# A two-layer transformer forward pass: small stages of layer two moved beside another product, bias rows written once, and fences parted

## The reference, cut to what matters

```python
h = rms_norm_2(x, ln1_w)
proj = h @ w_in                      # q 1024, six k/v of 256, gates 24, qkv 3072, z 1024, a 8, b 8, merge 4096
# compressed attention branch: 32 tokens flattened (+ position), two small matrices
blocks = blocks + pe
flat = blocks...reshape(b, n_cmp, g, CMP_BLOCK * dh)     # 15 blocks, 2 groups, 32*128 long
kc = jax.nn.gelu(flat_k @ w1_k) @ w2_k                   # hidden 256
vc = jax.nn.gelu(flat_v @ w1_v) @ w2_v
```

## Time and profile before

| | |
|---|---|
| Median of three executions | 3448.09 us |
| The profiled execution | 3446.6 us |
| Its span | 3444.8 us |
| TensorE busy | 3072.5 us, 89% of the span |
| VectorE, ScalarE busy | 1596.7 us, 1312.6 us |
| Mean granted TensorE clock | 0.926 of full |
| DMA moved | 519.30 MB, mean 151 GB/s |

### The profile page before, as it was taken

One profiled execution on the slowest core, in us unless ns is written; L12 is line 12 of the kernel. 1 busy time (PEld: TensorE's weight loads), 2 busy tenths in 40 slices (PEclk: granted clock), 3 DMA queues, 4 the chain that ended last, 5 costly groups with the idle time before them and its releaser, 6 DMA issues.

```text
span 3444.8 us, 36204 instructions
## 1 busy us (share of the span) xinstructions
PE 3072.5 (89%) x14022; PEld 2525.0 (73%) x14022; DVE 1596.7 (46%) x1648; ACT 1312.6 (38%) x1404; POOL 48.0 (1%) x89
## 2 busy tenths in 40 slices
PE   6798874998999999998997888799889999999997
PEld 5686554876887778776885676688768887888785
DVE  3332335455554445544424556444455544444443
ACT  3333231354443334434333334422233444334432
POOL 0001000000000000000001000000000000000000
PEclk9897775999999999999988999898999999999998
DMA  7643120543554455445525333222345555555553
GB/s 180 193 171 101 49 82 11 195 159 111 184 186 151 175 194 184 151 171 189 197 90 189 121 110 123 109 94 85 149 158 183 183 186 180 188 188 185 178 188 110
DMA packets 78180, 519.30 MB, mean 151 GB/s; under 512 B 10048, under 2 KB 10260, under 8 KB 24544
## 3 DMA queue, kind: packets, MB, share of 16 engines
q1 hardware_dynamic: 71280, 485.64, 39.2%
q0 software_dynamic: 6800, 32.28, 3.7%
HBM read 505.56 MB, written 12.32 MB: 150 GB/s over the span
## 4 chain that ended last, share of the span: by engine, by line
PE 82%; DVE 6%; ACT 4%; DMA 3%; issue 2%; DVEq 1%; ACTq 0%; another core or an unknown queue 0%; SPq 0%; POOL 0%; POOLq 0%; PEldq 0%
PE acc L282 24%; PE acc L284 23%; PE acc L283 23%; DMA w_raw<-in_w_win 2%; DVE w_lo L194 2%; PE wk L618 1%; ACT w_hi L189 1%; PE wk L649 1%; PE wk L1222 1%; PE wk L1128 1%; PE wk L1800 1%; PE wk L632 1%; ACT h_hi L441 1%; PE wk L1798 1%; PE wk L621 1%
## 5 line engine op out<-in xcount | busy, mean ns | idle before, releaser
L194 DVE TENSOR_TENSOR w_lo<-w_raw,w_hi 128x2048 fp32r<-128x2048 f32 (+2 forms) x492 | 1061.1, 2157 | 1257.9 <-ACT w_hi L189 1257.7
L189 ACT ACTIVATE w_hi<-w_raw 128x2048 fp32r<-128x2048 f32 (+2 forms) x492 | 889.2, 1808 | 1220.3 <-PE acc L284 1136.6
L282 PE MATMUL acc<-w_hi,h_hi 128*128 128x512 f32 x2656 | 1071.4, 403 | 102.1 <-DVE w_lo L194 45.7
L283 PE MATMUL acc<-w_lo,h_hi 128*128 128x512 f32 x2656 | 1055.1, 397 | 0.0
L284 PE MATMUL acc<-w_hi,h_lo 128*128 128x512 f32 x2656 | 1053.6, 397 | 0.0
L282 PEld LDWEIGHTS acc<-w_hi,h_hi 128*128 128x128 f32 x2656 | 515.1, 194 | 226.6 <-issue 64.2
L284 PEld LDWEIGHTS acc<-w_hi,h_lo 128*128 128x128 f32 x2656 | 513.9, 193 | 110.0
L283 PEld LDWEIGHTS acc<-w_lo,h_hi 128*128 128x128 f32 x2656 | 515.1, 194 | 104.0
L282 PE MATMUL acc<-w_hi,f_hi 128*128 128x512 f32 x856 | 341.5, 399 | 14.9 <-DVE x L330 7.0
L284 PE MATMUL acc<-w_hi,f_lo 128*128 128x512 f32 x856 | 339.6, 397 | 0.0
L283 PE MATMUL acc<-w_lo,f_hi 128*128 128x512 f32 x856 | 337.3, 394 | 0.0
(11 more groups left out here) (359 smaller groups left out, 2169.6 us busy)
## 6 DMA issues: line engine op xcount, KB each, us to landing
w_raw<-in_w_up_a SPq DMA_DIRECT2D x76, 1024.0 KB, 4.8
w_raw<-in_w_up_b SPq DMA_DIRECT2D x72, 1024.0 KB, 4.8
w_raw<-in_w_win SPq DMA_DIRECT2D x52, 1024.0 KB, 4.8
w_raw<-in_w_merge SPq DMA_DIRECT2D x32, 1024.0 KB, 4.8
w_raw<-in_w_down_a SPq DMA_DIRECT2D x32, 1024.0 KB, 4.8
w_raw<-in_w_down_b SPq DMA_DIRECT2D x32, 1024.0 KB, 4.8
w_raw<-in_w_win2g SPq DMA_DIRECT2D x24, 1024.0 KB, 4.8
w_raw<-in_w_down_a SPq DMA_DIRECT2D x24, 768.0 KB, 4.2
```

The source lines that it names most:

```text
L189: act_.activation(w_hi[:, s % SPL, 0:k], w_raw[:, s % RAW, 0:k], ACT.Copy).then_inc(hi_ready, 1)
L194: dve_.tensor_tensor(w_lo[:, s % SPL, 0:k], w_raw[:, s % RAW, 0:k], w_hi[:, s % SPL, 0:k].bitcast(F32), ALU.subtract).then_inc(lo_ready, 1)
L282: pe_.matmul(o, xh, wh, start=kt == 0, stop=False)
L283: pe_.matmul(o, xh, wl, start=False, stop=False)
```

## The change

It does these things:
- `win2` has the compression columns first (chunk 0), then q (chunks 1 and 2), then the other k (chunk 3) and v (chunk 4).
- `win2` is a Together with `small2`, the turning in three stages, and `flat` in two parts; the items after which the 9 parts stand are given by hand. `cmp_k`, `cmp_v` follow, in 4 items of the full 1 MB each. `z` comes behind them, beside `compress` in 3 parts.
- A fence is parted, in every Together: the signal is given when the last part of a small stage is done, the wait stands ahead of the first part of the next.
- A bias row is stored once in HBM, and a second DMA, HBM to HBM, makes the 128 copies, with 128 as its outer dimension and all heads in one row; the loads of `tri` and `cmask` stand between them.

```diff
-P2_Q, P2_KC, P2_VC, P2_KS, P2_KW, P2_VS, P2_VW = 0, 1024, 1280, 1536, 1792, 2048, 2304
+P2_KC, P2_VC, P2_Q, P2_KS, P2_KW, P2_VS, P2_VW = 0, 256, 512, 1536, 1792, 2048, 2304
...
-        ("win2", 5, four, CH), ("cmp_k", 1, split_counts(32, 8), CHID), ("cmp_v", 1, split_counts(32, 8), CHID),
-        ("win2g", 6, four, CH), ("z", 2, four, CH),
+        ("win2", 5, four, CH), ("cmp_k", 1, [8] * 4, CHID), ("cmp_v", 1, [8] * 4, CHID),
+        ("z", 2, four, CH), ("win2g", 6, four, CH),
...
-        toe1 = nc.dram_tensor("toe1_scratch", (A_H, P, TOE), F32, kind="Internal").ap()
-        toe2 = nc.dram_tensor("toe2_scratch", (N_H, P, TOE), F32, kind="Internal").ap()
+        row1 = nc.dram_tensor("toe1_rows", (A_H, TOE), F32, kind="Internal").ap()
+        row2 = nc.dram_tensor("toe2_rows", (N_H, TOE), F32, kind="Internal").ap()
+        toe1 = nc.dram_tensor("toe1_scratch", (P, A_H * TOE), F32, kind="Internal").ap()
+        toe2 = nc.dram_tensor("toe2_scratch", (P, N_H * TOE), F32, kind="Internal").ap()
...
+                self.slots = slots or [-(-(p + 1) * Q // self.parts) - 1 for p in range(self.parts)]
...
             def pieces(self, k, e):
                 for i, w in enumerate(self.work):
-                    yield from w.walk(k, e)
-
-                    e.drain().then_inc(fenced[k], 1)
                     for other in fenced:
-                        if other != k:
-                            e.wait_ge(fenced[other], self.base + i + 1)
+                        if i and other != k:
+                            e.wait_ge(fenced[other], self.base + i)
+                    parts = w.walk(k, e)
+                    for p in range(w.parts):
+                        next(parts)
+                        if p == w.parts - 1:
+                            for _ in parts:
+                                pass
+                            e.drain().then_inc(fenced[k], 1)
+                        yield
...
-                        g.pe_item(e, n, j, False)
+                        g.pe_item(e, n, j, n == 0)
...
-                        make(ahead[q + 1][0], e, ahead[q + 1][1], ahead[q + 1][2])
-                    while done < (q + 1) * self.parts // Q:
+                        if q or not g.norm:
+                            make(ahead[q + 1][0], e, ahead[q + 1][1], ahead[q + 1][2])
+                        if q == 1 and g.norm and k == "act":
+                            g.norm.root(e, 1)
+                        if q == 1 and g.norm and k == "dve":
+                            g.norm.inverse(e, 1).then_inc(scaled, 1)
+                    while done < self.parts and self.slots[done] <= q:
...
-            for table, row, heads in ((toe1, tsum[0], A_H), (toe2, tsum[1], N_H)):
-                e.dma_start(table, row.unsqueeze(1).to_broadcast([heads, P, TOE])).then_inc(toe_dma, 16)
-            e.wait_ge(toe_dma, 32)
+            for rows, row in ((row1, tsum[0]), (row2, tsum[1])):
+                e.dma_start(rows, row).then_inc(toe_rows, 16)
             load(e, "tri", tri[:], t_in["tri"])
             load(e, "cmask", cmask[:], t_in["cmask"])
+            e.wait_ge(toe_rows, 32)
+            for table, rows, heads in ((toe1, row1, A_H), (toe2, row2, N_H)):
+                every = bass.AP(tensor=rows.tensor, offset=0, ap=[[0, P], [1, heads * TOE]])
+                e.dma_start(table, every).then_inc(toe_dma, 16)
+            e.wait_ge(toe_dma, 32)
...
-                    src = bass.AP(tensor=table.tensor, offset=h * P * TOE + off, ap=[[TOE - 1, P], [1, w]])
+                    src = bass.AP(tensor=table.tensor, offset=h * TOE + off, ap=[[heads * TOE - 1, P], [1, w]])
...
-        stages.append(Gemm("win2", lhs, 0, *rows_to(p2, norm=ln1.norm)))
-        stages[-1].follows(ln1)
-        stages.append(spilled)
+        win2 = Gemm("win2", lhs, 0, *rows_to(p2, norm=ln1.norm))
+        win2.follows(ln1)
...
+        def turn2(name, chunk, first, tiles):
+            ...
+            def pe_after(e):
+                for t in range(TT):
+                    e.wait_ge(evac[t], win2.c + chunk + 1)
+                yield from pe(e)
...
-        stages.append(Together("small2+z", [Gemm("z", lhs, 0, *rows_to(z_rows, norm=ln1.norm))], [
-            small2, turn2, Steps("flat", None, flat_act, flat_dve)]))
+        stages.append(Together("win2+small2", [win2], [
+            small2, turn2("turn_kv_c", 0, P2_KC, range(8, 12)), Steps("flat", None, flat_act, flat_dve, 2),
+            turn2("turn_q", 2, P2_Q, range(0, 8)), turn2("turn_k", 3, P2_KS, range(12, 16))],
+            [4, 5, 6, 8, 9, 10, 13, 14, 17]))
+        stages.append(spilled)
...
-        stages.append(Steps("compress", cmp_pe, cmp_act, None))
+        stages.append(Together("z+compress", [Gemm("z", lhs, 0, *rows_to(z_rows, norm=ln1.norm))],
+                               [Steps("compress", cmp_pe, cmp_act, None, 3)], [0, 2, 4]))
```

More of the change, by code:

```diff
@@ L363, in build, with __init__ @@
         class Together:
-            def __init__(self, name, gemms, work, lead=0):
+            def __init__(self, name, gemms, work, slots=None):
                 self.name, self.gemms, self.work = name, gemms, work
@@ L370, in __init__ @@
                 self.parts = sum(w.parts for w in work)
-                self.lead = lead
+                Q = sum(g.n * g.ipc for g in gemms)
+                self.slots = slots or [-(-(p + 1) * Q // self.parts) - 1 for p in range(self.parts)]
+                assert len(self.slots) == self.parts and self.slots == sorted(self.slots)
                 self.base = fences[0]
@@ L389, in run @@
                 make = Gemm.make_hi if k == "act" else Gemm.make_lo
-                work, done, Q = self.pieces(k, e), 0, len(items)
+                work, done = self.pieces(k, e), 0
                 for q, (g, n, j) in enumerate(items):
                     if k == "pe":
-                        g.pe_item(e, n, j, False)
+                        g.pe_item(e, n, j, n == 0)
                     else:
@@ L1481, in build @@
         small2 = Steps("small2", small2_pe, small2_act, small2_dve, 3)
-        turn2 = Steps("turn2", *to_tiles([
-            ((lambda t, i=i: p2[:, t, i * P:(i + 1) * P]), tt2[:, i, :]) for i in range(16)]))
+        def turn2(name, chunk, first, tiles):
+            pe, act, dve, parts = to_tiles([
+                ((lambda t, c=first + i * P: p2[:, t, c:c + P]), tt2[:, tile, :]) for i, tile in enumerate(tiles)])
+            def pe_after(e):
+                for t in range(TT):
+                    e.wait_ge(evac[t], win2.c + chunk + 1)
+                yield from pe(e)
+            return Steps(name, pe_after if parts > 1 else lambda e: list(pe_after(e)), act if parts > 1 else lambda e: list(act(e)), dve, parts)
         after_turn2 = len(stages) + 1
@@ L1512, in flat_dve @@
                 if k:
+                    yield
+                if k:
                     e.wait_ge(f_hi_s, 2 * k)
@@ L1532, in flat_act @@
                 act_.activation(flat_hi[:, k * FW:(k + 1) * FW], lp2[:, 0:FW], ACT.Copy).then_inc(f_hi_s, 1)
+                if not k:
+                    yield
             act_.activation(flat_hi[:, 2 * FW:2048], lp2[:, 1100:1100 + 2048 - 2 * FW], ACT.Copy)
+            yield
         z_rows = x[:, :, 0:1024]
-        stages.append(Together("small2+z", [Gemm("z", lhs, 0, *rows_to(z_rows, norm=ln1.norm))], [
-            small2, turn2, Steps("flat", None, flat_act, flat_dve)]))
+        stages.append(Together("win2+small2", [win2], [
[3 more added lines that the diff above has]
+        stages.append(spilled)
         class Compress(Gemm):
@@ L2184, in layout @@
     mg = o[12]
-    weights("win2", cols(w, [(q, 1024), (kc, 256), (vc, 256), (ks, 256), (kw, 256), (vs, 256), (vw, 256)]))
+    weights("win2", cols(w, [(kc, 256), (vc, 256), (q, 1024), (ks, 256), (kw, 256), (vs, 256), (vw, 256)]))
     weights("win2g", cols(w, [(qkv, 3072)]))
```

3 lines of the change are left out of this document (2 added, 1 removed).

## The result

The changed kernel takes **3386.24 us** in the median of four executions (3382.98 to 3391.24); the kernel before, beside it on the same chip, 3447.24 us (3444.63 to 3448.18). The ratio is 0.9826, with a 95% interval from 0.9808 to 0.9843: 61 us less. The prediction was 3393 us, in a range of 3380 to 3414. The profiled execution took 3388.2 us with a span of 3386.3, which is 58.4 us less than the profiled execution before. Where they differ by a few microseconds, the traces of the other runs tell what comes back each time and what doesn't; experiment 7 has a second one of the changed kernel.

A forecast was written before the change was run, and what follows sets the result against it. TensorE, busy nine tenths of most slices, was taken as the bound, so only its waits or low clock could give time back. 3446.6 - 33 - 19 - 3 = 3391.6, with the median 1.5 us higher: 3393 us, range 3380 to 3414.

The forecast's parts named there:

- Bias rows: In `win`: 34.2 us lost while the bias rows were stored, less 1 us of stall, a gain of 33 us.
- rival 1: In `win`: the HBM to HBM copy still starves it, gain 12 instead of 33, 3414 us; chance 0.13.
- rival 3: In `win`: a copy from one row is served from one place in memory and runs longer, 3467 us; chance 0.03.
- The other sum of the prediction: Bias copy in `win`: 16 engines at an unchanged rate each, a copy of 53 us and a gain of 9.
- Layer two: From `win2` to `win2g`: moved small stages and full compression items gain 19 us, from 7 to 25.
- item 8: In `win2`: ScalarE does the last part of `small2` before rounding this item, a new wait losing 1.4 us.
- `flat`: Two parts behind items 9 and 10 of `win2`: waits of 2.6 and 2.1 us, net gain 5.4 us.
- clock: In `win2`: lower clock behind the three new waits, between nothing and 3 x 1.8 us, taken as 2.0 lost.
- compression products and `compress`: `cmp_k`, `cmp_v` in full items, 7.5 us a pair, gain 8.6 us; `compress` beside `z`, gain 2.9 us.
- sign of error: In the profile of layer two: `win2` longer than 157 us would show the forecast wrong.
- second price for the three waits: In `win2`: by the skill's clock rule each wait costs, 5.4 us instead of 2.0, and the sum is 3396.
- The fences elsewhere: Parted fences in `gdn+merge` (2.3 us there) and all other Togethers: 3 us together, bounds 0 and 8.

The follow-up runs named there:

- experiment 7: Changed kernel with `flat` in three parts instead of two: 3380.71 us; repeated on one chip 3380.03 us, beside the unedited changed kernel at 3385.25 us.
- experiment 4: Kernel before, bias rows stored once in HBM and copied from there in the old layout's 1.5 KB pieces, 128 outermost: 3413.43 us.
- experiment 5: Kernel before, bias rows stored once in HBM and copied from there in 1.5 KB pieces, the heads outermost: 3410.75 us.
- experiment 1: Kernel before with only the bias rows' part of the change: 3409.15 us, ratio 0.9894.
- experiment 3: Changed kernel with the old fences, signal and wait together ahead of the next small stage: 3389.94 us, ratio 0.9843.
- experiment 2: Kernel before with only the parted fences: 3436.10 us over ten executions, ratio 0.9972.

## Why the prediction was right, step by step

**Bias rows, 33 us predicted.** 34.5 in the trace, 37 by themselves in the runs. The sum said 1 us of stall, and there is none. The reason that I gave, long pieces and repeated reads of one row that aren't slow, needs mending. Pieces of 1.5 KB are as good when they come from HBM (experiments 4 and 5). I had weighed shape and traffic, and the source decided. So the size came out by a comparison with copies of another kind, and that is partly luck. Rivals 1 and 3 both priced the traffic at the HBM; it costs nothing here. The other sum of the prediction, 9 us of gain by the rule of the Trainium skill on the number of engines (DMA: Bandwidth & Descriptors, Why a DMA increments its semaphore by 16 and not by 1) and an unchanged rate of an engine, is far off, because the packets themselves became 3.7 times faster in experiment 5. (By the first store's rate, 2304 KB over 12 engines in 41.2 us, that sum gives 51.5 us for the copy and not 53, and rival 1's 54% is 0.56 in the row of `win2`; neither changes the argument.)

**Layer two, 19 us predicted, 17.1 in the trace.** By its terms:

| | predicted | trace |
|---|---|---|
| `win2`, `z` and `flat` (waits in `z` 5.3, item 8 -1.4, `flat` 5.4, clock -2.0) | 7.3 | 207.7 - 158.0 - 43.5 = 6.2 |
| compression products and `compress` (8.6 and 2.9) | 11.5 | 45.8 - 31.4 - 3.4 = 11.0 |

43.5 are `z`'s eight items and 3.4 the rest of its window. Item 8 waited 1.38 us against 1.4, item 11 2.85 against 2.6. Item 12 waited 0.35 and not 2.1, because item 11 ran slower: its 7.2 us at the lower clock gave VectorE 1.8 us more. In the second trace, at full clock, it waited 1.79. Wait and clock were not independent, as my sum had them: 2.85 + 0.35 + 1.8 = 5.0 us in one trace and 2.84 + 1.79 = 4.6 in the other stand against 2.6 + 2.1 and a part of 2.0. Experiment 7 takes 4.6 of them away in either pair and so shows what they were worth.

A pair of items in `cmp` took 7.49 us, from the second wait to the third here, where 7.5 were predicted:

```profile
1745.63 0.38 PE L284 MATMUL acc<-w_hi,oa_hi 128*128 128x256 f32 x1 [1.44 <-DVE w_lo L196]
1753.12 0.39 PE L284 MATMUL acc<-w_hi,oa_hi 128*128 128x256 f32 x1 [1.45 <-DVE w_lo L196]
```

That is the filling and the pair as foretold; both products took 31.4 us, just above the 31 that I had named.

What my sum had wrong is the length of the small product. I carried it over from one execution: with the 8-column matmuls 29.0 us to the next item, and 7.1 for that item. In the changed trace they took 31.0 and 8.2, which is why `win2` took 158.0 us, above the 157 that I had named as a sign of error; by the terms of my sum it was to take 155.3. The move is not the cause. In four other traces of the old place they took 31.4 to 32.3 us to the next item, in seven others of the new place 29.8 to 30.3. The 29.0 were the shortest of all thirteen. In the second trace of the changed kernel `win2` took 157.2. `z` with `compress` took 47.1 us in both, 1.5 less than the 48.6 of my sum, which hides a part of it. From the first matmul of `win2` to that of `win2g` were 253.3 us before, 256.5 to 257.3 in the three runs with only the bias rows changed, and 236.3 and 235.6 in the two traces of the changed kernel. So layer two's gain is 17 to 22 us by the pair of traces that one takes, and 19.2 by the medians of experiments 1 and 3.

**Rule and rows on the clock.** The prediction's second price for the three waits, 5.4 us, was my reading of the Trainium skill (TensorE: Matmul & The Clock Gate, Part 1: The HAM clock gate), which says that the throttled clock is the default and activity releases it; that each short wait pays, it doesn't say. It came out too high. Behind the wait of 1.38 us the clock is 1.00, and six waits of 0.6 to 1.5 us in `cmp` leave it at 1.00. Behind the wait of 2.85 us stands a low stretch, and behind the same wait of 2.84 us in the second trace none. That the clock falls where TensorE stands for long agrees with the old `flat` and `compress`, at 0.68 and 0.70; what a short wait costs can't be told from its length here.

**The fences elsewhere, 3 us.** From attention's end on the trace gives 1.2 us, but in that part 5.3 us are chance: the stretch from attention's end into `gdn+merge`, with the same code and the same waits of TensorE, took 121.9 us here, at a clock of 0.89, and 116.5 in the second trace of the changed kernel, at 0.95. Behind it the rows are steady (the two last lines of the table): together 404.0 to 404.5 us in the five traces with old fences, 401.2 to 401.6 in seven of the eight with the new ones and 403.1 in the eighth. Between the five and the seven that is 2.4 to 3.3 us, so the 3 us were right. What fell is the expectation of experiment 2, 3 to 5 us for the fences alone: it counted the next item's remainder made ahead of a drain, and left out what an earlier start of `flat` and Gelu, and a clock that stays up in `z`, bring where they stand in the open.

**What the sum lacked.** The start of `win2g`, 2 us. The pair of traces has 5.3 us between `win2g`'s first items and the end of attention: 194.5 us before and 189.2 now. Windows of `win2g`'s start and of the rest, before, then after:

```profile
1871.50:1884.00 12.50, 12.50 (x47) 10.13 (x48) 3.33 (x6) 5.69 (x7) 1.06 (x2) 0.81 0.29 100
1884.00:2066.00 182.00, 159.46 (x744) 129.62 (x743) 95.96 (x215) 70.80 (x145) 0.00 (x0) 0.92 0.32 116
```

```profile
1819.30:1830.00 10.70, 10.55 (x48) 8.81 (x49) 3.59 (x7) 5.70 (x7) 1.06 (x2) 1.00 0.55 202
1830.00:2008.50 178.50, 155.98 (x742) 127.14 (x741) 95.72 (x215) 70.76 (x145) 0.00 (x0) 0.94 0.33 118
```

1.8 us come from `win2g`'s start: in the old order it stood behind `compress` in the open and began at the lower clock. The other 3.5 go with a clock of 0.94 for 0.92 at equal work. Which of the two comes back shows in the lengths of the same stretches, from a start of `w_lo` to another, in us (the times are those of the kernel before):

| | before | experiments 1, 4, 5 | 2, fences alone | changed | changed, second trace | 3, old fences |
|---|---|---|---|---|---|---|
| layer two, 1596 to 1874 | 277.9 | 281.8, 282.4, 280.8 | 275.0 | 261.4 | 258.8 | 260.2 |
| `win2g`'s start, to 1884 | 9.9 | 10.2, 9.9, 9.1 | 9.9 | 7.8 | 7.9 | 8.0 |
| attention, to 2066 | 182.7 | 179.8, 182.7, 179.4 | 180.0 | 179.5 | 182.1 | 180.7 |
| start of `gdn+merge`, to 2187 | 120.9 | 120.8, 120.9, 119.1 | 119.5 | 121.9 | 116.5 | 116.4 |
| `gdn+merge`, to 2393 | 205.5 | 205.4, 205.5, 204.5 | 201.6 | 201.7 | 202.0 | 205.5 |
| its end and what follows, to 2591 | 198.6 | 198.6, 198.5, 200.0 | 199.6 | 199.9 | 199.4 | 198.9 |

The start of `win2g` is shorter in every trace of the new order. Attention is not: it takes 179.4 to 182.7 us in the old order and 179.0 to 185.3 in all eight traces of the new one. Its 3.5 us are chance of these two executions.

## What to carry to other kernels

When a transfer slows others, read its share of the engines' time against its bytes and packets, and change its source before its shape: a short row that is copied many times is stored once in HBM and copied from there. When a small stage moves beside a product, cost what stands behind it in each engine's program: the additions on VectorE were cheap, but ScalarE waited for them with an item behind it, and a cut of the parts that lets one engine run a part behind the other takes that away. A gain of two edits at the same place is counted once: the fences alone gave 9.7 us in the old order and about 4 in the new.

A stretch whose code no edit touches can differ by 3 to 5 us between two executions of one kernel, all of it clock. Before such a difference is given a cause, the same stretch is read in the traces of the other runs.

## What the runs showed of the hardware that I had not expected

A packet of GpSimd's queue took 0.47 us in the mean while the tables were stored out of rows in 12 and 8 on-chip partitions, and 0.127 us while they were copied out of HBM, with 1702 and 1712 packets and the same bytes.

An item at the lower clock hides the next engine's lateness: behind the same wait of 2.85 us the next one was 0.35 us after an item of 7.2 us, and 1.79 us where the clock stayed up.

The stretch below full clock at the 40-column product is not a fixed length, and its place alone doesn't set it: the same matmuls, with the item behind them, had 27.2 us of it in the kernel before and 34.1 to 34.2 in four other traces with the product in the same place; in the new place it was 34.2 us once and 30.6 to 30.8 in seven traces.
